# Residual joins in token halves: the last chunk, the norm, the residual steps and the next pair of chunks cut in two

## The reference

```python
for layer in range(2):
    x = x + rmsnorm(mixer(rmsnorm(x, mix_pre)), mix_post)
    x = x + rmsnorm(swiglu(rmsnorm(x, ffn_pre)), ffn_post)
# rmsnorm(y, g) = y / sqrt(mean(y * y over channels) + 1e-6) * g
```

## Time and profile before

| | before |
|---|---|
| median of 3 runs | 2880.47 us |
| lowest, highest | 2874.29, 2884.24 us |
| the profiled execution | 2879.64 us, its span 2877.8 us |
| mean granted TensorE clock | 0.957 of full |
| PE busy | 2670.4 us (93%) |
| PEld busy | 2369.0 us (82%) |
| DVE busy | 1318.3 us (46%) |
| ACT busy | 989.6 us (34%) |
| POOL busy | 1243.4 us (43%) |
| chain that ended last | PE 82%, DVE 8%, ACT 3%, issue 3%, POOL 2% |

### The profile page before, as it was taken

The page is one execution under the profiler, slowest core; times in us unless marked ns, Lnnn a source line. Parts: engine busy times, 40 slices in busy tenths (PEclk is TensorE's granted clock), DMA queues, the critical chain, the costliest instruction groups (busy, mean ns, idle before and its releaser), DMA issues.

```text
span 2877.8 us, 44613 instructions
## 1 busy us (share of the span) xinstructions
PE 2670.4 (93%) x15733; PEld 2369.0 (82%) x15733; DVE 1318.3 (46%) x1820; ACT 989.6 (34%) x1451; POOL 1243.4 (43%) x632
## 2 busy tenths in 40 slices
PE   7979767999999879999987899999999989999998
PEld 5769645888887768888865679999999989999997
DVE  2358666798787554312345633211234443220334
ACT  3242444432233345222235534222224334222221
POOL 4434233454554345544545314444443334543441
PEclk9989869999999999999999989999999989999998
DMA  5445111233332212333321121232232212232231
GB/s 127 95 132 114 61 40 35 66 100 98 93 108 76 73 55 70 95 102 95 99 84 63 43 81 57 82 92 69 84 88 69 75 47 59 80 87 78 84 90 53
DMA packets 451746, 230.10 MB, mean 80 GB/s; under 512 B 90588, under 2 KB 443568, under 8 KB 451127
## 3 DMA queue, kind: packets, MB, share of 16 engines
q1 hardware_dynamic: 451647, 228.80, 27.8%
HBM read 213.43 MB, written 15.43 MB: 80 GB/s over the span
## 4 chain that ended last, share of the span: by engine, by line
PE 82%; DVE 8%; ACT 3%; issue 3%; POOL 2%; DMA 0%; SPq 0%; DVEq 0%; ACTq 0%; POOLq 0%
PE psum L655 67%; PE psum L687 3%; PE psum L754 2%; DVE top L1795 1%; PE psum L895 1%; DVE scores L1802 1%; DVE probs_t L2011 1%; PE psum L787 1%; PE psum L976 1%; DVE row_stats L2000 1%; PE psum L771 1%; PE psum L983 1%; PE psum L966 1%; PE psum L824 1%; POOL act_split L1630 1%
## 5 line engine op out<-in xcount | busy, mean ns | idle before, releaser
L1598 POOL TENSOR_TENSOR w_lo<-w_raw,w_hi 128x1024 fp32r<-128x1024 f32 (+1 forms) x336 | 859.9, 2560 | 1263.5 <-ACT w_hi L1163 1263.5
L655 PE MATMUL psum<-act_split,w_hi 128*128 128x288 f32 (+1 forms) x6144 | 1363.8, 331 | 32.9 <-POOL w_lo L1598 11.9
L655 PEld LDWEIGHTS psum<-act_split,w_hi 128*128 128x128 f32 x6144 | 993.8, 190 | 128.3 <-issue 19.3
L1163 ACT ACTIVATE w_hi<-w_raw 128x1024 fp32r<-128x1024 f32 (+1 forms) x336 | 376.9, 1122 | 1390.3 <-PE psum L655 1348.5
L655 PE MATMUL psum<-act_split,w_lo 128*128 128x288 f32 (+1 forms) x3072 | 841.5, 328 | 0.0
L655 PEld LDWEIGHTS psum<-act_split,w_lo 128*128 128x128 f32 x3072 | 525.7, 190 | 40.8
L655 PE MATMUL psum<-hidden_split,w_hi 128*128 128x288 f32 (+1 forms) x2112 | 461.5, 327 | 0.0
L655 PEld LDWEIGHTS psum<-hidden_split,w_hi 128*128 128x128 f32 x2112 | 339.4, 188 | 27.5
L655 PE MATMUL psum<-hidden_split,w_lo 128*128 128x288 f32 (+1 forms) x1056 | 287.7, 327 | 0.0
L2070 DVE TENSOR_TENSOR temps<-psum,root_of_input 128x512 f32<-128x512 f32 (+1 forms) x88 | 63.5, 722 | 357.5 <-PE psum L655 344.8
L2076 DVE TENSOR_TENSOR temps<-psum,temps 128x512 f32<-128x512 f32 (+1 forms) x88 | 63.4, 721 | 350.7 <-PE psum L655 332.4
(11 more groups left out here) (253 smaller groups left out, 2411.9 us busy)
## 6 DMA issues: line engine op xcount, KB each, us to landing
w_raw<-in_w_ffn_gate_up SPq DMA_DIRECT2D x352, 256.0 KB, 3.1
w_raw<-in_w_ffn_down SPq DMA_DIRECT2D x64, 384.0 KB, 3.6
w_raw<-in_w_ffn_down SPq DMA_DIRECT2D x64, 320.0 KB, 4.0
w_raw<-in_w_in_even SPq DMA_DIRECT2D x64, 256.0 KB, 3.7
w_raw<-in_w_in_odd SPq DMA_DIRECT2D x64, 256.0 KB, 2.9
w_raw<-in_w_out_odd SPq DMA_DIRECT2D x32, 256.0 KB, 3.0
x_rows<-in_x_prompt SPq DMA_DIRECT2D x8, 512.0 KB, 5.9
w_raw<-in_w_out_even SPq DMA_DIRECT2D x32, 128.0 KB, 2.9
```

The source lines that it names most:

```text
L655: mm = pe.matmul(PS[:, 2 * p + b, 0:hi - lo], w[:, p, at], x(k)[:, lo:hi], start=(k == 0 and w is WH and x is x_hi), stop=(k == ph.kt - 1 ...
L1163: act.activation(WH[:, p, 0:n], WR[:, p, 0:n], ACT.Copy).then_inc(S("w_hi"), 1)
L1598: pool.tensor_tensor(WL[:, p, 0:n], WR[:, p, 0:n], WH[:, p, 0:n].bitcast(F32), ALU.subtract).then_inc(S("w_lo"), 1)
```

## The change

- **Last chunk.** `last_chunk` makes the last chunk of the phases ahead of a join one token half after the other (256 columns in g0, 288 in g1; before, g0 had one matmul of 512). Inside the second half stand the column sums and the spread of the first half. The last block's squares are made by ScalarE from each half into PSUM and added by VectorE to the sum of the seven others.
- **The next pair.** `join` replaces `post` and `first_pair` for s = 0, 1, 2. It goes by 13 units: channel blocks 0 to 3 of the first half, 0 to 3 of the second, blocks 4, 5, 6 whole, block 7 half by half. The first chunk follows the units; products of the second chunk are put between them, and more of them at the end. The sums and the spread of the second half stand at units 0 and 2. Four holds remain: one in unit 0, two in unit 1, one in unit 2. The column sums of the new squares are made at units 3, 3, 4, 5, 7, 9, 11 and between the last products; GpSimd adds three pairs of squares first.
- **Steps.** VectorE makes 16 half steps instead of 8, ScalarE and GpSimd follow by unit. With s = 3 the order is first half, then second, and `result` waits for each half.
- **Moved.** The high part of the next phase's second weight chunk goes from ScalarE to VectorE's `post` (a copy of 1024 columns), its low part on GpSimd is cut in two. The last root comes behind the next high part on ScalarE.
- **Top-k.** In `out` of g0 all sample rounds stand ahead of the seventh block add, three for each of the first blocks. The prompt's round behind the last `dn` chunk of the first feed-forward goes to `gate`, which now has three rounds instead of two.

The diff, cut to its core (indentation shortened, renumbering of semaphore counts left out):

```diff
+BOTH = 2
+UNITS = [(0, k) for k in range(4)] + [(1, k) for k in range(4)] + [(BOTH, k) for k in (4, 5, 6)] + [(0, 7), (1, 7)]
+NU = len(UNITS)
+STEPS = [(h, k) for h, k in UNITS[:8]] + [(h, k) for k in (4, 5, 6) for h in (0, 1)] + UNITS[11:]
+STEP_END = (1, 2, 3, 4, 5, 6, 7, 8, 10, 12, 14, 15, 16)
...
+def last_chunk(ph, x_hi, x_lo, s):
+    g, i = ph.g, ph.iters - 1
+    j = 4 * g + s
+    e = ph.free[1]
+    pe.wait_ge(S("w_lo"), ph.c0 + 2 * ph.iters)
+    pe.wait_ge(S(f"free_{e}1"), ph.base[e, 1] + i)
+    for h in (0, 1):
+        for k in range(ph.kt):
+            at = slice(P * k, P * k + P)
+            for w, x in ((WH, x_hi), (WH, x_lo), (WL, x_hi)):
+                mm = pe.matmul(PS[:, 2 + h, 0:HT[g]], w[:, 1, at], x(k)[:, part(h, g)],
+                               start=(k == 0 and w is WH and x is x_hi),
+                               stop=(k == ph.kt - 1 and w is WL))
+            if h and k == ph.kt // 3:
+                half_sums(g, s, 0)
+            if h and k == 2 * ph.kt // 3:
+                pe.wait_ge(S("n_rc"), r_at(g, SPOST[s]) + 1)
+                spread(0, g).then_inc(S("n_b"), 1)
+        mm.then_inc(S("w_used") if h else S("last_a"), 1)
+def half_sums(g, s, h):
+    j = 4 * g + s
+    if h:
+        pe.wait_ge(S("n_rt"), r_at(g, SPOST[s]) + 1)
+    pe.wait_ge(S("ss_last"), 2 * j + h + 1)
+    for k, lo, w in cells(h, g):
+        mm = pe.matmul(PS[0:w, 7, 2 * k:2 * k + 1], SS[:, lo:lo + w], ONES[:, 0:1], start=True, stop=True)
+    mm.then_inc(S("n_sum"), 1)
+def join(ph, s):
+    g = ph.g
+    j, m = 4 * g + s, 3 * g + s
+    r, r2 = r_at(g, SPOST[s]), r_at(g, SPRE[s])
...
+    first, second = ((WH, a_hi), (WL, a_hi)), ((WH, a_lo),)
+    def second_chunk(h, k):
+        return products(1, h, k, first + second)
+    def sums(u, sem, value):
+        pe.wait_ge(S(sem), value)
+        add_sums(square_at(u, g), UNITS[u][0], g).then_inc(S("sq_used"), 1)
...
+    for u, (h, k) in enumerate(UNITS):
+        pe.wait_ge(S("a_hi"), at + u + 1)
+        products(0, h, k, first)
+        if u == 0:
+            pe.wait_ge(S(f"free_{ph.prev[1][0]}1"), ph.prev[1][1])
+            hold(1)
+        if u == 1:
+            hold(1)
+        if u == 2:
+            pe.wait_ge(S("n_rc"), r + 2)
+            spread(1, g).then_inc(S("n_b"), 1)
+            hold(1)
+        if u == 3:
+            open_sums(g)
+            sums(0, "sq_m", NU * m + 1)
+            sums(1, "sq_m", NU * m + 2)
+        pe.wait_ge(S("a_lo"), at + u + 1)
+        mm = products(0, h, k, second)
+        if u == NU - 1:
+            mm.then_inc(S("w_used"), 1)
+        if u == 0:
+            half_sums(g, s, 1)
+        if u == 1:
+            hold(1)
+        if u == 4:
+            sums(2, "sq_m", NU * m + 3)
+            pair_free(ph, 1)
+            second_chunk(0, 0)
+        if u == 5:
+            sums(3, "sq_m", NU * m + 4)
+            second_chunk(0, 1)
+        if u == 6:
+            second_chunk(0, 2)
+            second_chunk(1, 0)
+        if u == 7:
+            sums(4, "sq_pair", 3 * m + 1)
+            second_chunk(0, 3)
+        if u == 8:
+            second_chunk(1, 1)
+            second_chunk(1, 2)
+        if u == 9:
+            sums(6, "sq_pair", 3 * m + 2)
+            second_chunk(1, 3)
+        if u == 11:
+            sums(8, "sq_pair", 3 * m + 3)
+    second_chunk(BOTH, 4)
+    sums(10, "sq_m", NU * m + 11)
+    second_chunk(BOTH, 5)
+    sums(11, "sq_m", NU * m + 12)
+    second_chunk(BOTH, 6)
+    sums(12, "sq_m", NU * m + 13)
+    close_sums(g).then_inc(S("n_sum"), 1)
+    second_chunk(0, 7)
+    pe.wait_ge(S("n_rc"), r2 + 1)
+    spread(BOTH, g).then_inc(S("n_b"), 1)
+    second_chunk(1, 7).then_inc(S("w_used"), 1)
...
+def last_block(g, s, h):
+    square = PS[:, 6 - h, 0:HT[g]]
+    if s in (0, 2):
+        act.wait_ge(*((S("w_used"), ph.c0 + NB) if h else (S("last_a"), j + 1)))
+        act.activation(square, PS[:, 2 + h, 0:HT[g]], ACT.Square).then_inc(S("sq_last"), 1)
+        act.activation(Y[:, NB - 1, part(h, g)], PS[:, 2 + h, 0:HT[g]], ACT.Copy).then_inc(
+            S(f"free_{e}1") if h else S("y_a"), 1)
+    else:
+        act.wait_ge(*((S(f"free_{e}1"), ph.end[e, 1]) if h else (S("y_a"), j + 1)))
+        act.activation(square, Y[:, NB - 1, part(h, g)], ACT.Square).then_inc(S("sq_last"), 1)
 def post(g, s):
-    root(r_at(g, SPOST[s]), g)
+    j, m = 4 * g + s, 3 * g + s
+    last_block(g, s, 0)
+    act.wait_ge(S("n_sum"), r_at(g, SPOST[s]) + 1)
+    root(0, g).then_inc(S("n_rt"), 1)
     if s == 3:
+        last_block(g, s, 1)
+        act.wait_ge(S("n_sum"), r_at(g, SPOST[s]) + 2)
+        root(1, g).then_inc(S("n_rt"), 1)
+        if g == 0:
+            hi_part(phase("out", 1), 0, 1)
         return
+    base, layer = ((G_FFN_PRE, 0), (G_MIX_PRE, 1), (G_FFN_PRE, 1))[s]
     nxt = (phase("gu", g), phase("v", g), phase("gu", g, 1))[s]
+    def square(u):
+        h, n = UNITS[u]
+        wait(act, S("sq_used"), 10 * m + (0 if u < 8 else 4 if u < 10 else 6))
+        act.activation(square_at(u, g), X[:, n, part(h, g)], ACT.Square).then_inc(S("sq_m"), 1)
+    for u, (h, n) in enumerate(UNITS):
+        act.wait_ge(S("x_new"), 16 * j + STEP_END[u])
+        act.activation(AR[:, 0, n, part(h, g)], X[:, n, part(h, g)], ACT.Identity, scale=gain(base, layer, n)).then_inc(S("a_hi"), 1)
+        act.activation(Y[:, n, part(h, g)], X[:, n, part(h, g)], ACT.Identity, scale=gain(base, layer, n)).then_inc(S("u_gx"), 1)
+        if u == 0:
+            last_block(g, s, 1)
+        if u == 1:
+            act.wait_ge(S("n_sum"), r_at(g, SPOST[s]) + 2)
+            root(1, g).then_inc(S("n_rt"), 1)
+        if u:
+            square(u - 1)
+    square(NU - 1)
     act.wait_ge(S("w_used"), nxt.c0 + 1)
     hi_part(nxt, 1, 0)
+    root_all(r_at(g, SPRE[s]), g)
     act.wait_ge(S("n_b"), r_at(g, SPRE[s]) + 1)
...
+    def low(u):
+        h, n = UNITS[u]
+        at = part(h, g)
+        pool.wait_ge(S("u_gx"), NU * m + u + 1)
+        pool.tensor_tensor(AR[:, 1, n, at], Y[:, n, at], AR[:, 0, n, at].bitcast(F32), ALU.subtract).then_inc(S("a_lo"), 1)
+    def weights(half):
+        at = slice(512 * half, 512 * half + 512)
+        pool.wait_ge(S("w_hi"), nxt.c0 + 2)
+        ins_ = pool.tensor_tensor(WL[:, 1, at], WR[:, 1, at], WH[:, 1, at].bitcast(F32), ALU.subtract)
+        if half:
+            ins_.then_inc(S("w_lo"), 1)
+    def add(u):
+        pool.wait_ge(S("sq_m"), NU * m + u + 2)
+        pool.tensor_tensor(square_at(u, g), square_at(u, g), square_at(u + 1, g), ALU.add).then_inc(S("sq_pair"), 1)
+    for u in range(NU):
+        low(u)
+        if u == 1:
+            weights(0)
+        if u == 3:
+            weights(1)
+        if u == 6:
+            add(4)
+        if u == 8:
+            add(6)
+        if u == 10:
+            add(8)
...
     add_square(mp, NB - 2, 0, g, z)
-    if extra:
-        extra(ph.iters - 1, 0)
-        extra(ph.iters - 1, 1)
...
-    total(NB - 1, 1)
-    if first is not None:
-        top_round(big, first + ph.iters - 1)
...
+    def total(h):
+        if s in (1, 3):
+            dve.wait_ge(*((S("w_used"), ph.c0 + NB) if h else (S("last_a"), j + 1)))
+            y = Y[:, NB - 1, part(h, g)]
+            dve.tensor_tensor(y, PS[:, 2 + h, 0:HT[g]], y, ALU.add).then_inc(S("free_d1") if h else S("y_a"), 1)
+    def add_last(h):
+        if h == 0:
+            dve.wait_ge(S("ss_p"), 7 * (norm_at("post", g, s) + 1))
+        dve.wait_ge(S("sq_last"), 2 * j + h + 1)
+        dve.tensor_tensor(SS[:, part(h, g)], PS[:, 6 - h, 0:HT[g]], SS[:, part(h, g)], ALU.add).then_inc(S("ss_last"), 1)
+    def step(i):
+        h, n = steps[i]
+        t = PS[:, 6, 0:HT[g]]
+        if i:
+            dve.wait_ge(S("x_new"), 16 * j + i)
+        dve.tensor_tensor(t, Y[:, n, part(h, g)], PS[:, 4 + h, 0:HT[g]], ALU.mult).then_inc(S("x_t"), 1)
+        dve.wait_ge(S("x_t"), 16 * j + i + 1)
+        x = X[:, n, part(h, g)]
+        dve.scalar_tensor_tensor(out=x, in0=t, scalar=gain(base, layer, n), in1=x, op0=ALU.mult, op1=ALU.add).then_inc(S("x_new"), 1)
+    total(0)
+    add_last(0)
+    half_inverse(g, s, 0)
     if g and s == 0:
         dve.wait_ge(S("xb_in"), 16)
+    dve.wait_ge(S("n_b"), r_at(g, SPOST[s]) + 1)
+    dve.wait_ge(S("y_a"), j + 1)
+    dve.wait_ge(S(f"free_{ph.free[0]}0"), ph.end[ph.free[0], 0])
+    step(0)
+    total(1)
+    step(1)
+    add_last(1)
+    if s < 3:
+        nxt = (phase("gu", g), phase("v", g), phase("gu", g, 1))[s]
+        dve.wait_ge(S("w_used"), ph.c0 + NB)
+        dve.wait_ge(S("w_hi"), nxt.c0 + 1)
+        dve.wait_ge(S("w_in1"), nxt.win[1] + 16 * nxt.nd)
+        dve.tensor_copy(WH[:, 1, 0:D], WR[:, 1, 0:D]).then_inc(S("w_hi"), 1)
+    step(2)
+    half_inverse(g, s, 1)
+    step(3)
+    for i in range(4, 16):
+        if steps[i] == (1, 0):
+            dve.wait_ge(S("n_b"), r_at(g, SPOST[s]) + 2)
+            dve.wait_ge(S(f"free_{ph.free[1]}1"), ph.end[ph.free[1], 1])
+        step(i)
+    if s < 3:
```

(20 more changed lines are left out.)

362 lines of the change are left out of this document (181 added, 181 removed).

## The result

The changed kernel takes 2909.71 us (median of 4 runs, 2901.51 to 2913.8) where the kernel before takes 2879.47. The ratio, estimated over the runs, is 1.0100, 95% interval [1.0084, 1.0116]. It is slower by 1%. Four more runs at the end of the study gave 2902.76 and a ratio of 1.0095 [1.0067, 1.0124]. The profiled execution took 2901.51 us, its span 2899.7, which is 21.9 more than the span of before. Its mean granted TensorE clock is 0.944 against 0.957: at two levels, 0.5 and 1, that is (1 - 0.944) x 2 x 2899.7 = 325 us at 1.2 GHz, against 247.

What follows compares the result with a forecast made beforehand. Streaming matmuls on TensorE bound most of the kernel and stay unchanged, so only joins (-6.3) and results (-7.6) gain: -13.9 us from 2879.64 makes 2865.7, forecast 2866.6 against the median, range 2852 to 2880.

Steps and rivals of the forecast that it cites:

- The results: After each group's last feed-forward: halving takes 16 transposes from the end, -3.5 us in g0 and -4.1 in g1.
- The joins: Six stretches between two matmul streams, three per token group: halving by tokens and moved top-k rounds give -6.3 us together.
- rival C: Slower: TensorE stops at almost every unit, the clock falls to 1.2 GHz in six tails; 2906 us, chance 0.10.
- g1 s1: Second group's join after the first feed-forward: 32.8 us from last chunk's end to second pair's first matmul, against 33.8; -1.0.
- g0 s1: First group's join after the first feed-forward: round removed, first spread 4.3 us after the last chunk's end; -0.7 us.
- g0 s0: First group's join after `out`: -1.8 us with some 6 us saved over seven adds, +4.1 without that saving.
- Rival B: Three engines within 2 us: handovers cost 1.2 us in five joins, g0 s0's adds save nothing; 2878.5, chance 0.24.
- Rival D: Faster joins: VectorE and ScalarE don't lag, a third of TensorE's 5 us a join is won; 2856.6, chance 0.13.
- The copy on VectorE: High part of the weights, 1024 columns, in VectorE's queue in a join: taken as 1.2 us, range from 0.7.
- the half steps: VectorE in the joins, 288 columns: 1.05 us each against 1.65 full; 16 take 16.7 us against 13.2.
- the 22.3 us to the low part of unit 11: GpSimd in a join: second-last low part ends 22.4 us after the first half's spread.
- the transposes: End of the results: 9 left in g0 and 17 in g1, after 16 of 25 and 16 of 33 move earlier.

Runs made afterwards that it cites:

- e5_widesums: Changed kernel with every column-sum matmul writing 64 equal columns instead of one, nothing else altered: 2886.5 us, ratio to before 1.0033.
- e6_widebefore: Kernel before with 64 equal columns instead of one in each column-sum matmul: 2881.0 us, ratio to before 1.0011.
- e7_topk: Kernel before with only the top-k rounds moved, joins and results as they were: 2871.5 us, ratio to before 0.9975.
- e9_topk_results: Kernel before with the moved top-k rounds and the results in halves, six joins as before: 2865.1 us, ratio to before 0.9951.
- e10_addlate: Changed kernel with 64-column sums, GpSimd's last addition of squares moved behind the last low parts, its column sums into the tail: 2885.9 us.
- e1_holds: Changed kernel with eight added matmuls of constants in each join, where TensorE waits for GpSimd's low parts: 2899.5 us, ratio to before 1.0059.
- e11_noholds_wide: Kernel before without the matmuls of constants in its post steps and with 64 columns in each column sum: 2899.1 us, ratio to before 1.0074.

## Why the prediction was wrong

Forecast -13.9 us, measured +30 by the first medians, +23 by the second and +21.9 in the profile. By stretches:

- **The results, -7.6 forecast.** Measured -3.05 and -3.2 from the start of the last chunk to the end of the stretch, -6.3 in all. Right, slightly too large: 9 and 17 records remain as forecast, and TensorE waits 0.5 us for each of the last steps.
- **The joins, -6.3 forecast, +26.2 measured.** With the clock held (`e5_widesums`) the same lines add to +10.0, some 3 of them the price of wide sums (an estimate from `e6_widebefore`: 2.1 by the medians, 3.2 by the ratio). So of the 32.5 us between forecast and measurement about 19 are the clock and 13 are terms.
- **The step that failed** is the clock, which the sum put at nothing by the sentence against rival C: "four holds are spread over the first units, and TensorE still works 24.6 of 31 us". I took busy time for what holds the clock. A set of sums counts as 1.34 us of work, in 12 records of one column each. In the old order 12 products stand between two sets of sums, 8 and 6 ahead of the last two; in the new tail six stand between sets of 1.34, 0.65 and 0.65 us, because the products that could have stood there had been used up to fill pauses. What the runs showed in its place: the clock at 1.2 GHz for 128 us of these lines instead of 63, and 56 once the sums have 64 columns. That the order of the tail, and not something else in the join, is what set off the falls is argued; shown is that the width of the sums decides. Rival C had the size (up to 6.6 us a join) and 0.10; its cause, the pauses, was not the main one. On the evidence of the earlier trace rows, a clock at 0.71 with TensorE busy 3.00 of 3.00 us, it deserved far more: that row already said that busy time does not hold the clock. Its number, 2906, came close by luck: it had six fallen tails and no error in the terms, where the trace has three or four falls and 13 us in terms.
- **Terms, +1.7 in g1 s1.** With the clock at 1.00 the first step is at T + 0.8 (0.1 forecast), the three sets of sums at their narrow width are 2.6 (2.2: six tiles in two halves, where the old five-tile set of the earlier trace rows was scaled), the spread is 2.02 with its wait (1.4), and the rest as worked. The sum for g1 s1 is then +0.7 instead of -1.0; `e5_widesums` has +1.5, 0.8 of it the wider sums of the tail. For the other joins this was not worked out.
- **g0 s1, -0.7 forecast.** The step was t0 = T + 4.3. The changed kernel has its first multiply at T + 5.8 (921.68 us, the chunk having begun at 908.35), and TensorE is stopped inside its last chunk (timeline, 907 to 922 us):

```profile
917.70 0.61 PE L785 MATMUL psum<-constants,square_sums 128*128 128x1 f32 x4 [3.80 <-DVE square_sums L2341]
```

  VectorE is still in the round of the pair of chunks before, until 914.4 us, so the first half's sum comes late, and TensorE, which used to run through the chunk meanwhile, now waits for it in the middle. Moving the rounds alone shortens this line of the table by 4.4 us; with the halved join nothing of it is left.
- **g0 s0, -1.8 forecast**, -3.8 with the clock held. The saving of 6 us that I assumed for adds and rounds is real in the main (4.1 us in `e7_topk`; the 7.0 of `e9_topk_results` are had with no time at 1.2 GHz on that line), but it belongs to the rounds, not to the halves.
- **Rival B** was half right. Several engines within 2 us of each other is what `e10_addlate` shows, and the 1.7 us of terms in g1 s1 are near its 1.2 a join; that the adds of g0 s0 save nothing is refuted by `e7_topk`. **Rival D** had nothing for it: 0.13 was wasted.
- The copy on VectorE, the half steps, the 22.3 us to the low part of unit 11, the transposes: right.

What stays open: how the +4.4, +1.8 and +4.0 us of g0 s2, g1 s0 and g1 s2 with wide sums divide between the terms and the dips that remain on those lines (6, 8 and 7 us at 1.2 GHz, against 0, 12 and 3 in the kernel before). `e10_addlate` has +3.1, +0.9 and +2.5 there, with 3, 6 and 3 us. A version with wide sums in the tail alone was not tried.

## What to carry to other kernels

Before filling TensorE's pauses with work pulled forward, look at what is left for the end: here a tail with many one-column matmuls let the clock fall, in `e1_holds` with no idle time left ahead of it, and the fall cost the start of the next stream too. Widening the moving operand of such matmuls is nearly free and is the cheapest test of it. And when a change has several parts, build the small ones alone: here two of them were worth 14 us, and the large one cost 38 to 45.

## What the runs showed of the hardware

- The busy time of the profile did not tell whether the granted clock would fall: 2.00 of 2.00 us busy and a fall in `e1_holds`, 0.67 of 2.00 busy and none in `e5_widesums`. Sixty-four columns instead of one in each matmul of sums, and nothing else, brought the mean clock from 0.936 to 0.944 up to 0.949 to 0.959.
- A matmul with 64 moving columns of float32 costs little more than one with a single column: 12 records in 1.60 us against 1.34. I had expected no difference.
- Matmul time itself has a small second value. In the profile of `e11_noholds_wide` the line "stream and g1 s1" is 436.8 us, though 7 us of it are at 1.2 GHz, against 443.4 to 446.0 in the kernels whose clock is 1.00 on all of it. The streams of `e7_topk` and `e11_noholds_wide` by form:

```profile
L655 PE MATMUL psum<-act_split,w_hi 128*128 128x288 f32 x1314 | 228.5, 296 | 0.0
```

```profile
L655 PE MATMUL psum<-act_split,w_hi 128*128 128x288 f32 x1344 | 229.0, 292 | 0.9 <-DVE temps L2068 0.9
```

  4 ns a record; the whole stream takes 399.7 us instead of 409.9. The cause is not known. It may be behind single runs that lie 10 us or more under their median (2856.9 in `e7_topk`, median 2871.5); no profile of such a run shows it.
